# A chunked RWKV-7 scan: GpSimd's mask of the backward inverse levels behind VectorE's running sums, and y of the backward direction on the other two quadrants of TensorE's array

## The chip, the cores and the metric

One NeuronCore of a Trainium2 chip runs the whole program. It has five engines with queues of their own: TensorE (PE in the profile, its weight loads PEld), VectorE (DVE), ScalarE (ACT), GpSimd (POOL) and SyncE (SP), which here only issues DMAs. Engines meet through semaphores. The metric is the device time of the program in microseconds, lower is better.

## What is computed

The reference is an encoder trunk of two layers over 1280 tokens (a prompt of 1024 and a sample of 256) of width 1024: neighbourhood attention, a gated MLP, an RWKV-7 time mixing in both directions, and a second gated MLP. The change lies in the scan of the time mixing. For each of 16 heads of 64 channels and each direction a state S (64 x 64) goes through the tokens:

```python
def _wkv7_step(S, inp):
    r_t, w_t, k_t, v_t, aa_t, bb_t = inp
    sa = jnp.einsum('zbhij,zbhj->zbhi', S, aa_t)
    S = S * w_t[..., None, :] + sa[..., :, None] * bb_t[..., None, :] + v_t[..., :, None] * k_t[..., None, :]
    y = jnp.einsum('zbhij,zbhj->zbhi', S, r_t)
    return S, y
```

z is the direction, forward (0) or backward (1); y of both is added later, in the gate.

## The kernel before

The scan is the function `rwkv_scan`. Two heads make a pair, on partitions 0 to 63 and 64 to 127 (`halves`); there are 8 pairs. The tokens are cut in chunks of C = 64, and U = 4 chunks of each direction make a **group** of W = 256 tokens, 5 to a pair, so NG = 40 groups. For a chunk the recurrence is solved in closed form: products of decayed keys and queries (`gram`), the inverse of a triangular 64 x 64 matrix, built level by level (`inverse`), and then the chain that must go from chunk to chunk: `x_product`, `u_product`, `s_product`, which gives the next state `st`. When a group's chain is done, `y_products` gives y of all its chunks.

Each engine has a hand-written program: a loop over I from -3 (or -4) to NG - 1, in four steps s each. In loop I the chain of group I runs, the inverse of group I + 1, gram and the level masks of group I + 2, decays and keys of group I + 3, and y of group I - 1. One turn of this loop is called a loop here. Every engine does its instructions in the order in which they are issued; only semaphores order engines against each other. What matters for the change, in step s = 1 of a loop:

- TensorE: x, inverse level, u, inverse level, s, `gram` of group I + 2 for z = 1, then `y_products(I - 1)` (L1681 on, matmuls at L1693, L1695 and L1697), then an inverse level. In step 2: x, an inverse level, u, `turn` (transposes of keys and values), and an inverse level that needs the level output of VectorE (L1952).
- VectorE: level outputs, the state output (L1967), `gram_out` for z = 1 (L1912 writes `bm`, which frees GpSimd's mask), a level output, then `sums(I + 3)`: the running sums over the log decays of a group, forward (L1851) and backward (L1852), and L1855 and L1856, which turn the backward one around. L1856 signals `d_cum`. The next level output follows it.
- ScalarE: waits for `d_cum` and takes exponentials (L1769, L1770); it copies y from PSUM (`y_copy`, L1804) and the inverse's products (L1781).
- GpSimd: `directions(I + 3)` (L2000, L2002), `levels(I + 2, 1)` in step 2 (L2019, L2026, L2027), `receptance(I + 3)` in step 3 (L2009, L2010), `bonus_add` (L2036). `levels(G, z)` multiplies the gram block `bm` by the mask of level 0 (L2019), adds the identity (L2026), and multiplies `bm` by the masks of the other five levels, 128 x 1280 elements (L2027), for TensorE's inverse in the next loop.
- SP: loads of a group, then the stores of y (`store_y`, L1514), one DMA for each direction.

A head's matmul of 64 x 64 takes one quadrant of the 128 x 128 array: its input half gives the row half, its output half the column half. y of both directions went from half h to half h, and `y_ps` has one PSUM bank for each z. `side(h, z)` is half h for z = 0 and the other half for z = 1. An fp32 matmul of this kind is two records in the trace.

Of the kernel before, what the change touches and what calls it, by code (L numbers as in the profile page):

```python
# [15 lines left out]
ALU = mybir.AluOpType  # L16
# [3 lines left out]
P = 128  # L20
# [1334 lines left out]
C = 64  # L1355
# [4 lines left out]
Z = 2  # L1360
# [13 lines left out]
def rwkv_scan(nc, rkvl, kks, w0, w2, a0, a2, k_a, r_k, ysc, bsc, consts):  # L1374

    U = 4
    W = U * C
    NS = T // W
    NG = PAIRS * NS
    INV = LEVELS - 1  # L1380
    halves = (slice(0, HD), slice(HD, P))
    with Phase(nc, "sc") as ph:
        ident = ph.sb("ident", [P, P])
        block64 = ph.sb("block64", [P, P])
        eye2 = ph.sb("eye2", [P, Z, C])
# [30 lines left out]
        rec = ph.sb("rec", [P, 4, Z, U, 4, C])  # L1416
        yt = ph.sb("yt", [P, 3, Z, W])
# [10 lines left out]
        nr = ph.sb("nr", [P, 4, Z, 2, U, C])  # L1428
        t0 = ph.sb("t0", [P, 2, Z, 2, U, C])
        vt = ph.sb("vt", [P, 2, Z, U, C])  # L1430
        xs = ph.sb("xs", [P, Z, C])
        tu = ph.sb("tu", [P, 2 * U, Z, C])
        st = ph.sb("st", [P, 2 * U, Z, C])
# [8 lines left out]
        y_ps = low_ps[:, :, 0:W]  # L1442
# [4 lines left out]
        y_stored, b_stored = ph.sems("y_stored", 3), ph.sems("b_stored", 2)  # L1447
# [5 lines left out]
        d_start, d_cum, d_run, d_tb, d_rec, d_bonus, d_two, d_st, a_y = (  # L1453
            ph.sem(x) for x in ("d_start", "d_cum", "d_run", "d_tb", "d_rec", "d_bonus", "d_two", "d_st", "a_y"))
        d_bm, d_gram, d_first, d_t, d_r = (ph.sems(x, Z) for x in ("d_bm", "d_gram", "d_first", "d_t", "d_r"))
        g_kd, g_ab, g_r, g_bt = (ph.sem(x) for x in ("g_kd", "g_ab", "g_r", "g_bt"))
        g_bl, g_r0, g_first = (ph.sems(x, Z) for x in ("g_bl", "g_r0", "g_first"))

        def col_of(z, j):
            return (j if z == 0 else NS - 1 - j) * W  # L1460

        def unit(z, s):
            return s if z == 0 else U - 1 - s

        def group(G):
            return 0 <= G < NG

        def side(h, z):
            return halves[h] if z == 0 else halves[1 - h]
# [8 lines left out]
        with nc.Block() as block:  # L1478
            @block.sync
            def _(sp):  # L1480
                loads = [(ident[:], consts["ident"]), (block64[:], consts["block64"]), (eye2[:], consts["eye2"]),
                         (m_strict[:], consts["m_strict"]), (m_incl[:], consts["m_incl"]), (m_level[:], consts["m_level"]),
                         (keep[:], consts["keep"]), (wa[:, 0], w2), (wa[:, 1], a2)]
                with nc.allow_non_contiguous_dma("parameters by channel"):
                    for i, q in enumerate((w0[0], w0[1], a0[0], a0[1], k_a, r_k)):
                        sp.dma_start(prm[:, i], q.rearrange("(k p) -> p k", p=P)).then_inc(small_in, 16)
                for dst, src in loads:
                    sp.dma_start(dst, src).then_inc(small_in, 16)

                def load(G):  # L1490
                    p, j = divmod(G, NS)
                    s = G % 2
                    if G >= 2:
                        sp.wait_ge(g_r, G - 1)
                        sp.wait_ge(d_rec, G - 1)
                    for z, rows in enumerate(halves):
                        c = col_of(z, j)
                        sp.dma_start(low[rows, s], rkvl[rows, 3 * KT:3 * KT + 2, c:c + W]).then_inc(s_in[s], 16)
                        sp.dma_start(rk[:, s, :, z], rkvl[:, p:p + KT + 1:KT, c:c + W]).then_inc(s_in[s], 16)
                        sp.dma_start(kk[:, s, z], kks[:, p, c:c + W]).then_inc(s_in[s], 16)  # L1500
                    if G >= 4:
                        for z in range(Z):
                            sp.wait_ge(pe_turn[z], G - 3)
                        sp.wait_ge(d_bonus, G - 3)
                    for z in range(Z):
                        c = col_of(z, j)
                        sp.dma_start(vb[:, G % 4, z], rkvl[:, 2 * KT + p, c:c + W]).then_inc(v_in[G % 4], 16)

                def store_y(G):
                    p, j = divmod(G, NS)  # L1510
                    sp.wait_ge(a_y, G + 1)
                    for z in range(Z):
                        c = col_of(z, j)
                        sp.dma_start(ysc[:, p, z, c:c + W], yt[:, G % 3, z]).then_inc(y_stored[G % 3], 16)  # L1514

                for I in range(-4, NG):
                    if group(I + 4):
                        load(I + 4)
                    if I >= 2 and I % NS == 2:
                        p = I // NS  # L1520
                        sp.wait_ge(d_bonus, (p + 1) * NS)
                        sp.wait_ge(g_bt, (p + 1) * 2)
                        sp.wait_ge(d_two, p + 1)
                        sp.dma_start(bsc[:, p], bt[:, p % 2]).then_inc(b_stored[p % 2], 16)
                    if I >= 2:
                        store_y(I - 2)
                store_y(NG - 2)
                store_y(NG - 1)
                for s in range(3):
                    sp.wait_ge(y_stored[s], 32 * len(range(s, NG, 3)))  # L1530
                for s in range(2):
                    sp.wait_ge(b_stored[s], 16 * PAIRS // 2)

            @block.tensor
            def _(pe):
# [145 lines left out]
                def y_products(G):  # L1681
                    pe.wait_ge(a_u, 4 * G + 4)
                    if group(G + 4):
                        pe.wait_ge(a_tanh, G + 5)
                    else:
                        pe.wait_ge(d_bonus, NG)
                        pe.wait_ge(a_turn[0], min(G + 2, NG))
                    for z in range(Z):
                        for s in range(U):
                            u, g = unit(z, s), (4 * G + s) % (2 * U)  # L1690
                            to = slice(u * C, (u + 1) * C)
                            for rows in halves:
                                nc.tensor.matmul(y_ps[rows, z, to], st[rows, g, z], rec[rows, G % 4, z, u, 3], start=True, stop=False)  # L1693
                            for rows in halves:
                                nc.tensor.matmul(y_ps[rows, z, to], tu[rows, g, z], nr[rows, G % 4, z, 0, s], start=False, stop=False)  # L1695
                            for rows in halves:
                                last = nc.tensor.matmul(y_ps[rows, z, to], vt[rows, G % 2, z, s], nr[rows, G % 4, z, 1, s], start=False, stop=True)  # L1697
                    last.then_inc(pe_y, 1)

                def bonus(G):  # L1700
# [34 lines left out]
            def _(act):  # L1735
# [64 lines left out]
                def y_copy(G):  # L1800
                    act.wait_ge(pe_y, G + 1)
                    if G >= 3:
                        act.wait_ge(y_stored[G % 3], 32 * (G // 3))
                    nc.scalar.activation(yt[:, G % 3], y_ps, ACT.Copy).then_inc(a_y, 1)  # L1804

                for I in range(-3, NG):
# [184 lines left out]
            def _(pool):  # L1991
# [17 lines left out]
                    nc.gpsimd.tensor_tensor(rec[:, G % 4, :, :, 0], uc(ab[:]), uc(ex2[:]), ALU.mult)  # L2009
                    nc.gpsimd.tensor_tensor(rec[:, G % 4, :, :, 3], uc(rk[:, G % 2, 0]), ex1_of, ALU.mult).then_inc(g_r, 1)  # L2010

                def levels(G, z):
                    pool.wait_ge(d_bm[z], G + 1)
                    if z == 0 and G >= 3:
                        pool.wait_ge(pe_u, 4 * G - 8)
                    if z == 1 and G >= 1:
                        pool.wait_ge(d_start, G)
                    first = rf[:, G % 3, 0] if z == 0 else r0[:]
                    nc.gpsimd.tensor_tensor(first, bm[:, z], m_level[:, 0, z:z + 1].to_broadcast([P, U, C]), ALU.mult).then_inc(g_first[z], 1)  # L2019
                    if G >= 2:  # L2020
                        pool.wait_ge(pe_p[z], 5 * G - 5)
                    m = m_level[:, 1:LEVELS, z]
                    mask = strided(m, 0, [[Z * C, INV], [0, U], [1, C]])
                    src = strided(bm[:, z], 0, [[0, INV], [C, U], [1, C]])
                    pool.wait_ge(g_first[z], G + 1)
                    nc.gpsimd.tensor_tensor(first, first, eye2[:, z:z + 1].to_broadcast([P, U, C]), ALU.add).then_inc(g_r0[z], 1)  # L2026
                    nc.gpsimd.tensor_tensor(bl[:, G % 2, z], src, mask, ALU.mult).then_inc(g_bl[z], 1)  # L2027

                def bonus_add(G):
# [9 lines left out]
                for I in range(-3, NG):  # L2039
                    for s in range(U):  # L2040
                        if s == 1 and group(I + 2):
                            levels(I + 2, 0)
                        if s == 2 and group(I + 2):
                            levels(I + 2, 1)
                        if s == 1 and group(I + 3):
                            directions(I + 3)
                        if s == 3 and group(I + 3):
                            receptance(I + 3)
                        if s == 0 and group(I + 2):
                            bonus_add(I + 2)  # L2050
# [320 lines left out]
```

## Time and profile before

| | before |
|---|---|
| median of 3 runs (lowest, highest) | 4919.04 us (4917.08, 4932.63) |
| profiled execution, its own time | 4925.97 us |
| its span, first to last instruction | 4924.0 us |
| TensorE, VectorE, ScalarE, GpSimd busy | 4368.1, 1982.0, 1291.8, 1276.4 us |
| mean granted TensorE clock | 0.947 |

Times in the rows are microseconds from the span's start unless marked ns. A timeline row gives start, duration, engine, line, operation, output and inputs, and the count of instructions merged in it; in brackets stands the idle time of the engine before it, with what ended that. "issue" is time in which the engine waited for nothing that the profile shows.

### The profile page before, as it was taken

The numbers are of one execution on the slowest core, as the hardware profiler recorded it, in microseconds if no ns is written. First come the engines' busy times: TensorE is split into PE (matmuls) and PEld (weight loads), VectorE is DVE, ScalarE is ACT, GpSimd is POOL, SyncE is SP. The second block draws the span as 40 slices with busy tenths as digits, with TensorE's granted clock in tenths as the row PEclk, the third lists the DMA queues.
The fourth block names the chain that finished last, engine by engine and source line by source line (L and its number), as shares of the span: only waits on it lengthen the run. The fifth ranks groups of instructions, "written<-read, shape, count | busy, mean of one in ns | idle before, by whom it ended". The sixth has DMA issues, their size and how long they took to land. (4 is left out here: it accounts for less than half of the span.)

```text
span 4924.0 us, 112761 instructions
## 1 busy us (share of the span) xinstructions
PE 4368.1 (89%) x50312; PEld 3680.4 (75%) x50312; DVE 1982.0 (40%) x3380; ACT 1291.8 (26%) x2542; POOL 1276.4 (26%) x794
## 2 busy tenths in 40 slices
PE   3899798999999996997948888888878999999997
PEld 2788766888888885876747777777765888888886
DVE  3011064253242533125156666666644244153341
ACT  2111075211110112335124444444422211011110
POOL 2111132311111124111045445445422321111110
PEclk6899999999999997998979999999999999999998
DMA  3211243312213122221231122121222411312214
GB/s 129 66 58 60 79 118 80 109 39 66 93 39 125 39 78 60 75 70 60 78 86 61 60 73 61 60 69 59 63 77 96 126 40 41 123 39 89 70 48 165
DMA packets 401998, 372.41 MB, mean 76 GB/s; under 512 B 62416, under 2 KB 369872, under 8 KB 399344
## 3 DMA queue, kind: packets, MB, share of 16 engines
q1 hardware_dynamic: 389680, 354.75, 23.2%
q10 hardware_dynamic: 11840, 10.49, 0.6%
q8 instruction: 397, 6.50, 0.6%
q14 instruction: 81, 0.66, 0.0%
HBM read 257.68 MB, written 107.48 MB: 74 GB/s over the span
## 5 line engine op out<-in xcount | busy, mean ns | idle before, releaser
L422 POOL TENSOR_TENSOR f_wlow<-f_raw,f_whigh 128x1024 fp32r<-128x1024 f32 (+1 forms) x152 | 360.1, 2369 | 1670.9 <-ACT f_whigh L493 1670.9
L478 PE MATMUL f_ps<-fx_hh,f_whigh 128*128 128x512 f32 (+1 forms) x2112 | 529.8, 359 | 0.0
L478 PE MATMUL f_ps<-fx_hl,f_whigh 128*128 128x512 f32 (+1 forms) x2112 | 528.7, 358 | 0.0
L478 PE MATMUL f_ps<-fx_hh,f_wlow 128*128 128x512 f32 (+1 forms) x2112 | 528.5, 358 | 0.0
L1603 PE MATMUL sc_inv_ps<-sc_tf,sc_bl 64*64 64x64 f32 x6400 | 281.0, 224 | 158.8 <-DVE sc_tf L1952 120.6
L493 ACT ACTIVATE f_whigh<-f_raw 128x1024 fp32r<-128x1024 f32 (+1 forms) x152 | 156.5, 1030 | 923.2 <-PE f_ps L478 894.9
L478 PEld LDWEIGHTS f_ps<-fx_hl,f_whigh 128*128 128x128 f32 x2112 | 349.1, 189 | 65.3
L478 PEld LDWEIGHTS f_ps<-fx_hh,f_whigh 128*128 128x128 f32 x2112 | 349.4, 189 | 64.7
L478 PEld LDWEIGHTS f_ps<-fx_hh,f_wlow 128*128 128x128 f32 x2112 | 348.8, 189 | 65.2
L478 PE MATMUL f_ps<-mo_oh,f_whigh 128*128 128x512 f32 (+1 forms) x1440 | 360.8, 359 | 25.9 <-POOL f_wlow L422 25.9
L1603 PEld LDWEIGHTS sc_inv_ps<-sc_tf,sc_bl 64*64 64x64 f32 x6400 | 235.6, 136 | 196.8 <-issue 111.6
L478 PE MATMUL f_ps<-mo_ol,f_whigh 128*128 128x512 f32 (+1 forms) x1440 | 360.3, 359 | 0.0
L478 PE MATMUL f_ps<-mo_oh,f_wlow 128*128 128x512 f32 (+1 forms) x1440 | 360.0, 358 | 0.0
L547 DVE TENSOR_TENSOR f_xo<-f_ps,f_xo 128x512 f32<-128x512 f32 x168 | 90.8, 596 | 619.0 <-PE f_ps L478 586.9
L478 PEld LDWEIGHTS f_ps<-mo_oh,f_whigh 128*128 128x128 f32 x1440 | 240.2, 189 | 69.3 <-POOL f_wlow L422 26.6
L478 PEld LDWEIGHTS f_ps<-mo_ol,f_whigh 128*128 128x128 f32 x1440 | 240.2, 188 | 42.7
L478 PEld LDWEIGHTS f_ps<-mo_oh,f_wlow 128*128 128x128 f32 x1440 | 240.0, 188 | 42.9
L1206 PE MATMUL ri_ps<-ri_xh,ri_whigh 128*128 128x512 f32 (+1 forms) x672 | 185.0, 386 | 75.9 <-DVE ri_xl L1322 74.4
L1614 PE MATMUL sc_inv_ps<-sc_pt,sc_rf 64*64 64x64 f32 x5120 | 232.9, 227 | 7.3 <-issue 7.0
L2027 POOL TENSOR_TENSOR sc_bl<-sc_bm,sc_m_level 128x1280 f32<-128x1280 f32 x80 | 233.4, 2918 | 0.0
L1781 ACT ACTIVATE sc_pt<-sc_inv_ps 128x256 f32<-128x256 f32 x320 | 122.8, 384 | 383.0 <-PE sc_inv_ps L1603 382.6
L1206 PEld LDWEIGHTS ri_ps<-ri_xh,ri_whigh 128*128 128x128 f32 x672 | 117.9, 200 | 112.0 <-DVE ri_xl L1322 57.6
(268 smaller groups left out, 8688.4 us busy)
## 6 DMA issues: line engine op xcount, KB each, us to landing
f_xo<-xres SPq DMA_DIRECT2D x64, 640.0 KB, 4.0
xres<-f_xo SPq DMA_DIRECT2D x56, 640.0 KB, 2.9
f_raw<-in_ffn_w_gate SPq DMA_DIRECT2D x44, 512.0 KB
f_raw<-in_ffn_w_up SPq DMA_DIRECT2D x44, 512.0 KB
sc_rk<-rkvl SPq DMA_DIRECT2D x80, 256.0 KB, 3.3
rkvl<-ri_ot SPq DMA_DIRECT2D x28, 640.0 KB, 2.9
f_raw<-in_ffn_w_down SPq DMA_DIRECT2D x32, 448.0 KB
qkv_raw<-in_na_w_qkv SPq DMA_DIRECT2D x24, 512.0 KB, 5.7
```

The costliest lines, as they stand in the source:

```text
L422: nc.gpsimd.tensor_tensor(wlow[:, m % 2, 0:kt], raw[:, 0:kt], whigh[:, m % 2, 0:kt].bitcast(F32), ALU.subtract).then_inc(cut_lo, 1)
L478: last = nc.tensor.matmul(ps[:, m % 2, n, 0:count], w[:, m % 2, k], x[:, k, t0:t0 + count], start=(k == 0 and w is whigh and x is xh), sto ...
L493: nc.scalar.activation(whigh[:, m % 2, 0:kt], raw[:, 0:kt], ACT.Copy).then_inc(cut_hi, 1)
L547: last = nc.vector.tensor_tensor(dst, src, old, ALU.add)
L1206: last = nc.tensor.matmul(ps[:, m % 2, q, 0:count], w[:, m % 2, k], src[:, k, t0:t0 + count], start=(k == 0 and w is whigh and src is xh), ...
L1603: return nc.tensor.matmul(p_ps[z][side(h, z), s * C:(s + 1) * C], bl[rows, G % 2, z, k, s], tf[rows, G % 2, z, s], start=True, stop=True)
L1614: return nc.tensor.matmul(t_ps[z][halves[h], s * C:(s + 1) * C], rf[rows, G % 3, z, s], pt[rows, z, s], start=True, stop=True)
L1781: nc.scalar.activation(dst, src, ACT.Copy).then_inc(a_pt[z], 1)
L2027: nc.gpsimd.tensor_tensor(bl[:, G % 2, z], src, mask, ALU.mult).then_inc(g_bl[z], 1)
```

## The change

In the GpSimd program `levels` is split. `first_level` holds the product of level 0 and the addition of the identity, at the place they had. What is left of `levels`, the mask of the five other levels, waits for z = 1 on `d_cum` of the group whose sums VectorE takes in the same loop; for z = 0 it has no new wait.

In the TensorE program y of direction 1 is written to the other half than it is read from (`side(h, z)`), and the two directions are issued in turn, chunk by chunk, term by term and half by half. ScalarE's copy is as before, so y of direction 1 stands in `yt` with its halves exchanged, and SP stores it in two DMAs of 64 partitions; the counts of `y_stored` go from 32 to 48.

```diff
--- before.py
+++ after.py
@@ -1509,9 +1509,11 @@
                 def store_y(G):
                     p, j = divmod(G, NS)
                     sp.wait_ge(a_y, G + 1)
-                    for z in range(Z):
-                        c = col_of(z, j)
-                        sp.dma_start(ysc[:, p, z, c:c + W], yt[:, G % 3, z]).then_inc(y_stored[G % 3], 16)
+                    c = col_of(0, j)
+                    sp.dma_start(ysc[:, p, 0, c:c + W], yt[:, G % 3, 0]).then_inc(y_stored[G % 3], 16)
+                    c = col_of(1, j)
+                    for h, rows in enumerate(halves):
+                        sp.dma_start(ysc[rows, p, 1, c:c + W], yt[side(h, 1), G % 3, 1]).then_inc(y_stored[G % 3], 16)
 
                 for I in range(-4, NG):
                     if group(I + 4):
@@ -1527,7 +1529,7 @@
                 store_y(NG - 2)
                 store_y(NG - 1)
                 for s in range(3):
-                    sp.wait_ge(y_stored[s], 32 * len(range(s, NG, 3)))
+                    sp.wait_ge(y_stored[s], 48 * len(range(s, NG, 3)))
                 for s in range(2):
                     sp.wait_ge(b_stored[s], 16 * PAIRS // 2)
 
@@ -1685,16 +1687,18 @@
                     else:
                         pe.wait_ge(d_bonus, NG)
                         pe.wait_ge(a_turn[0], min(G + 2, NG))
-                    for z in range(Z):
-                        for s in range(U):
-                            u, g = unit(z, s), (4 * G + s) % (2 * U)
-                            to = slice(u * C, (u + 1) * C)
-                            for rows in halves:
-                                nc.tensor.matmul(y_ps[rows, z, to], st[rows, g, z], rec[rows, G % 4, z, u, 3], start=True, stop=False)
-                            for rows in halves:
-                                nc.tensor.matmul(y_ps[rows, z, to], tu[rows, g, z], nr[rows, G % 4, z, 0, s], start=False, stop=False)
-                            for rows in halves:
-                                last = nc.tensor.matmul(y_ps[rows, z, to], vt[rows, G % 2, z, s], nr[rows, G % 4, z, 1, s], start=False, stop=True)
+                    for s in range(U):
+                        g = (4 * G + s) % (2 * U)
+                        to = [slice(unit(z, s) * C, (unit(z, s) + 1) * C) for z in range(Z)]
+                        for h, rows in enumerate(halves):
+                            for z in range(Z):
+                                nc.tensor.matmul(y_ps[side(h, z), z, to[z]], st[rows, g, z], rec[rows, G % 4, z, unit(z, s), 3], start=True, stop=False)
+                        for h, rows in enumerate(halves):
+                            for z in range(Z):
+                                nc.tensor.matmul(y_ps[side(h, z), z, to[z]], tu[rows, g, z], nr[rows, G % 4, z, 0, s], start=False, stop=False)
+                        for h, rows in enumerate(halves):
+                            for z in range(Z):
+                                last = nc.tensor.matmul(y_ps[side(h, z), z, to[z]], vt[rows, G % 2, z, s], nr[rows, G % 4, z, 1, s], start=False, stop=True)
                     last.then_inc(pe_y, 1)
 
                 def bonus(G):
@@ -1800,7 +1804,7 @@
                 def y_copy(G):
                     act.wait_ge(pe_y, G + 1)
                     if G >= 3:
-                        act.wait_ge(y_stored[G % 3], 32 * (G // 3))
+                        act.wait_ge(y_stored[G % 3], 48 * (G // 3))
                     nc.scalar.activation(yt[:, G % 3], y_ps, ACT.Copy).then_inc(a_y, 1)
 
                 for I in range(-3, NG):
@@ -2009,7 +2013,7 @@
                     nc.gpsimd.tensor_tensor(rec[:, G % 4, :, :, 0], uc(ab[:]), uc(ex2[:]), ALU.mult)
                     nc.gpsimd.tensor_tensor(rec[:, G % 4, :, :, 3], uc(rk[:, G % 2, 0]), ex1_of, ALU.mult).then_inc(g_r, 1)
 
-                def levels(G, z):
+                def first_level(G, z):
                     pool.wait_ge(d_bm[z], G + 1)
                     if z == 0 and G >= 3:
                         pool.wait_ge(pe_u, 4 * G - 8)
@@ -2017,13 +2021,17 @@
                         pool.wait_ge(d_start, G)
                     first = rf[:, G % 3, 0] if z == 0 else r0[:]
                     nc.gpsimd.tensor_tensor(first, bm[:, z], m_level[:, 0, z:z + 1].to_broadcast([P, U, C]), ALU.mult).then_inc(g_first[z], 1)
+                    pool.wait_ge(g_first[z], G + 1)
+                    nc.gpsimd.tensor_tensor(first, first, eye2[:, z:z + 1].to_broadcast([P, U, C]), ALU.add).then_inc(g_r0[z], 1)
+
+                def levels(G, z):
                     if G >= 2:
                         pool.wait_ge(pe_p[z], 5 * G - 5)
+                    if z == 1 and group(G + 1):
+                        pool.wait_ge(d_cum, G + 2)
                     m = m_level[:, 1:LEVELS, z]
                     mask = strided(m, 0, [[Z * C, INV], [0, U], [1, C]])
                     src = strided(bm[:, z], 0, [[0, INV], [C, U], [1, C]])
-                    pool.wait_ge(g_first[z], G + 1)
-                    nc.gpsimd.tensor_tensor(first, first, eye2[:, z:z + 1].to_broadcast([P, U, C]), ALU.add).then_inc(g_r0[z], 1)
                     nc.gpsimd.tensor_tensor(bl[:, G % 2, z], src, mask, ALU.mult).then_inc(g_bl[z], 1)
 
                 def bonus_add(G):
@@ -2039,8 +2047,10 @@
                 for I in range(-3, NG):
                     for s in range(U):
                         if s == 1 and group(I + 2):
+                            first_level(I + 2, 0)
                             levels(I + 2, 0)
                         if s == 2 and group(I + 2):
+                            first_level(I + 2, 1)
                             levels(I + 2, 1)
                         if s == 1 and group(I + 3):
                             directions(I + 3)
```

## Rows read from the trace of the kernel before

**Rows 1.** The page, busy us (share) and instructions of each engine: TensorE's.

```profile
PE 4368.1 (89%) x50312; PEld 3680.4 (75%) x50312; DVE 1982.0 (40%) x3380; ACT 1291.8 (26%) x2542; POOL 1276.4 (26%) x794
```

**Rows 2.** Busy time by stretch, the scan stage; its header row names the columns.

```profile
2472.00:3670.00 1198.00, 953.68 (x31200) 870.44 (x31200) 776.09 (x1825) 471.82 (x1281) 567.48 (x432) 0.96 0.21 62
```

**Rows 3.** VectorE timeline, one late loop: start us, us, engine, line, operation [idle before].

```profile
3045.83 2.88 DVE L1851 TENSOR_TENSOR_SCAN sc_cum<-sc_restart,sc_sg 128x256 f32<-128x256 f32 x1
3048.64 0.66 DVE L1852 TENSOR_TENSOR_SCAN sc_run<-sc_restart,sc_sg 128x256 f32<-128x256 f32 x1
...
3049.41 0.41 DVE L1856 TENSOR_TENSOR sc_cum<-sc_run 128x252 f32<-128x252 f32 x1
3049.74 0.28 DVE L1952 TENSOR_TENSOR sc_tf<-sc_inv_ps,sc_tf 128x128 f32<-128x128 f32 x1
```

**Rows 4.** GpSimd timeline, the same loop.

```profile
3043.71 0.72 POOL L2019 TENSOR_TENSOR sc_r<-sc_bm,sc_m_level 128x256 f32<-128x256 f32 x1
3044.58 0.73 POOL L2026 TENSOR_TENSOR sc_r<-sc_r,sc_eye 128x256 f32<-128x256 f32 x1
3045.27 2.89 POOL L2027 TENSOR_TENSOR sc_bl<-sc_bm,sc_m_level 128x1280 f32<-128x1280 f32 x1
3052.63 1.27 POOL L2009 TENSOR_TENSOR sc_rec<-sc_ab,sc_ex 128x512 f32<-128x512 f32 x1 [4.46 <-ACT sc_exb L1770]
3053.86 1.19 POOL L2010 TENSOR_TENSOR sc_rec<-sc_rk,sc_exb 128x512 f32<-128x512 f32 x1
```

**Rows 5.** TensorE timeline, the same loop: where it resumes behind the sums.

```profile
3050.17 0.27 PE L1603 MATMUL sc_inv_ps<-sc_tf,sc_bl 64*64 64x64 f32 x2 [2.38 <-DVE sc_tf L1952]
```

**Rows 6.** Groups by line, VectorE, scan stage: xcount | busy us, mean ns | idle before.

```profile
L1851 DVE TENSOR_TENSOR_SCAN sc_cum<-sc_restart,sc_sg 128x256 f32<-128x256 f32 x40 | 89.8, 2245 | 9.6 <-ACT sc_sg L1755 9.6
...
L1852 DVE TENSOR_TENSOR_SCAN sc_run<-sc_restart,sc_sg 128x256 f32<-128x256 f32 x40 | 30.5, 763 | 0.0
```

**Rows 7.** Groups by line, VectorE, scan stage: the level outputs.

```profile
L1952 DVE TENSOR_TENSOR sc_tf<-sc_inv_ps,sc_tf 128x128 f32<-128x128 f32 x320 | 92.7, 290 | 234.8 <-PE sc_inv_ps L1614 232.4
```

**Rows 8.** VectorE and GpSimd timelines, the fourth loop.

```profile
2566.57 3.31 DVE L1852 TENSOR_TENSOR_SCAN sc_run<-sc_restart,sc_sg 128x256 f32<-128x256 f32 x1
...
2566.05 3.27 POOL L2027 TENSOR_TENSOR sc_bl<-sc_bm,sc_m_level 128x1280 f32<-128x1280 f32 x1
```

**Rows 9.** VectorE timeline: L1851 in the fifth loop and in the last.

```profile
2593.72 2.88 DVE L1851 TENSOR_TENSOR_SCAN sc_cum<-sc_restart,sc_sg 128x256 f32<-128x256 f32 x1
...
3590.32 2.89 DVE L1851 TENSOR_TENSOR_SCAN sc_cum<-sc_restart,sc_sg 128x256 f32<-128x256 f32 x1
```

**Rows 10.** VectorE timeline, the last loop.

```profile
3593.91 0.41 DVE L1856 TENSOR_TENSOR sc_cum<-sc_run 128x252 f32<-128x252 f32 x1
...
3599.29 0.75 DVE L1864 SCALAR_TENSOR_TENSOR sc_tb<-sc_kd,sc_prm,sc_rk 128x512 f32<-128x512 f32 x1
```

**Rows 11.** TensorE timeline: the first and the last start of one y block.

```profile
3041.64 0.31 PE L1693 MATMUL sc_low_ps<-sc_rec,sc_st 64*64 64x64 f32 x4
...
3044.41 0.22 PE L1697 MATMUL sc_low_ps<-sc_nr,sc_vt 64*64 64x64 f32 x1
```

**Rows 12.** TensorE timeline: an inverse level, first row, and what starts behind it.

```profile
3037.45 0.27 PE L1603 MATMUL sc_inv_ps<-sc_tf,sc_bl 64*64 64x64 f32 x2 [1.05 <-DVE sc_tf L1952]
...
3037.94 0.28 PE L1664 MATMUL sc_chain_ps<-sc_xs,sc_rf 64*64 64x64 f32 x5
```

**Rows 13.** TensorE timeline: the u products of one step.

```profile
3030.94 0.34 PE L1664 MATMUL sc_chain_ps<-sc_xs,sc_rf 64*64 64x64 f32 x8
```

**Rows 14.** Groups by line, TensorE, scan stage: L1603 with its idle time before.

```profile
L1603 PE MATMUL sc_inv_ps<-sc_tf,sc_bl 64*64 64x64 f32 x6400 | 281.0, 224 | 158.8 <-DVE sc_tf L1952 120.6 <-ACT sc_pt L1781 15.0 <-issue 11.5
```

**Rows 15.** TensorE timeline: a stop for issue.

```profile
3012.91 0.38 PE L1678 MATMUL sc_chain_ps<-sc_tu,sc_t 64*64 64x64 f32 x5 [1.02 <-issue]
```

**Rows 16.** One tile's instructions, sc_yt: its stores.

```profile
L1514 SPq DMA_DIRECT2D ysc<-sc_yt x80: 319/432/1956, 2611.5 to 3667.8; - x80
```

**Rows 17.** Waits of SP in the scan stage: waited for: us in total, times, longest us.

```profile
SPq L1495 <- DVE sc_pc L1879: 816.9, 38, 25.7
```

## The prediction, made before the change was run

> **What bounds the kernel now.** I read the page's busy shares first. TensorE is busy 4368.1 of 4924.0 us [rows 1], so a gain must come from TensorE's own work or from its waits. The diff touches only the scan stage (functions inside `rwkv_scan`), so the second view was the busy time by stretch: the scan runs from about 2472 to 3670 us. In those 1198 us TensorE is busy 953.68 at a granted clock of 0.96, and GpSimd is busy 567.48 [rows 2]. About 244 us of the stage are TensorE's idle time.
>
> The third view was the timeline of one late loop, engine by engine. VectorE's first running sum (L1851) stands there with 2.88 us, the second (L1852), the same operation on the same shape, with 0.66 [rows 3]. GpSimd's mask L2027 runs from 3045.27 to 3048.16 [rows 4], and the sum ends at 3048.71, 0.55 us behind it. In each of the 36 loops from the fifth on, the first sum ends 0.54 or 0.55 us after the end of the backward mask, whatever its own start was. So the sum does not run slowly: it stands still while the mask runs. The reader is to see who waits for that. Behind the sums VectorE has L1855, L1856 and the level output L1952 (3049.74), and TensorE resumes at 3050.17 after 2.38 us of idle time that the profile puts on that L1952 [rows 3, 5]. In all 36 loops TensorE resumes 0.34 to 0.36 us after L1856 ends. The wait is on the path.
>
> **Part 1, the mask behind the sums.** The product for level 0 and the addition of the identity (L2019, L2026) keep their place; only L2027 for z = 1 now waits for `d_cum`, which L1856 signals. The first sum has a mean of 2245 ns in 40 runs, the second 763 [rows 6]; clear of GpSimd either takes some 0.66, as L1852 in [rows 3]. The time that goes is 40 x (2.245 - 0.66) + 40 x (0.763 - 0.66) = 63.4 + 4.1 = **67 us**.
>
> Three things are taken off.
> (a) A new clash. With y shorter (part 2) the sum is ready about 1.3 us earlier, at 3045.83 - 1.30 = 3044.53. That is between L2019, which ends at 3044.43, and L2026, which starts at 3044.58 and ends at 3045.31 [rows 4]. The one case of that sort in the trace is the fourth loop: L2027 starts while a first sum runs and is stretched to 3.27 us, and the second sum then stands for 3.31 us, to 0.56 us behind it [rows 8]. Here the second GpSimd operation is only 0.73 long. The first sum ends at 3044.53 + 0.66 = 3045.19; L2026 begins its work about 0.22 before that, as in [rows 8] (a mask of 2.9 us that ends 3.27 behind 2566.05 has its work from 2566.42, and that sum ends at 2566.64), and ends near 3045.7; the second sum ends 0.55 later, 3046.25, against 3045.85 undisturbed: some 0.4 lost. If L2026 gets in first, the loss is 0.7. A first sum lasts 3.44 us less what it starts behind the mask, so with a start 1.30 earlier it meets L2026 where it lasts over 2.14 us now: 23 of the 36 loops, the first and the last among them [rows 9]; 18 at 0.4 and 5 at less, about -9 us.
> The Trainium skill (SBUF — State Buffer, "Who interferes with whom") says that a VectorE instruction with two SBUF inputs and a GpSimd instruction that reads SBUF lock each other out for the whole instruction, and that the one issued first keeps the ports. For VectorE as the loser [rows 3] agree with 2.88 against 0.66 us, for GpSimd as the loser [rows 8] with 3.27 against 2.89; by that rule the first sum would win in this clash and the loss be the 0.4.
> (b) In the first four loops other work still sets the pace, and in some late ones TensorE's wait is a little shorter than the excess (1.95 against 2.2 in one): I take -5 us.
> (c) GpSimd is now busy later. The mask runs from the end of L1856 + 0.1 to + 3.0; the receptance pair L2009, L2010 started 2.81 us after L1856 before (3052.63 against 3049.82) and takes 3055.05 - 3052.63 = 2.42 us [rows 3, 4], so it ends at + 5.45 instead of + 5.23 or, in the fast loops, 4.98. L1864, with two SBUF inputs as the sums have, begins at + 4.97 in the last loop (3599.29 against 3594.32) [rows 10], and within + 5.4 in 21 of the 36. There it will stand until 0.61 behind L2010, ending at 6.06 instead of 5.72: 0.34 x 21 = -7 us, by the 0.55 that the sum of [rows 3] ends behind the mask and 0.06 for the longer operation, because VectorE has no pause from there to the state output that TensorE waits for.
> Nothing else is queued badly: what is behind the new wait on GpSimd is the receptance, which needs exponentials that need `d_cum` anyway, and the mask itself is wanted by TensorE only in the next loop (`inverse(G, 1)`), behind L1864 and all of [rows 4]. The VectorE operations that the mask now lies beside (L1952, the transposes, L1967) have one SBUF input; over half of the 320 L1952 lie beside GpSimd work already, and their mean is 290 ns against the 0.28 of one that doesn't [rows 7, 3]. Part 1: 67 - 9 - 5 - 7 = **46 us**.
>
> **Part 2, y on four quadrants.** A group has 4 chunks x 2 directions x 3 terms x 2 halves = 48 matmuls of 64 x 64, 96 records. Before, each z used only the two diagonal quadrants, and in one loop the block goes from 3041.64 to the last start at 3044.41 [rows 11]: 2.77 us, 28.9 ns a record. Where two z are issued together on all four quadrants, the inverse levels have 32 records from 3037.45 to 3037.94 [rows 12], 15.3 ns each; the u products have 8 in 0.34 us where one alone takes 0.22 [rows 13, 11], so (0.34 - 0.22) / 7 = 17.1 ns. So y takes 96 x 15.3 = 1.47 us (saving 1.30) or 1.64 (saving 1.13). I take 1.30, since the inverse runs as long a row of them: 40 blocks, **52 us**, lower bound 45. No wait lies between gram, y and the next inverse level, so all of it is on TensorE's path, and what follows (ACT's copy of y and of p, then L1952, then the sum) moves up with it; it is this that makes clash (a).
>
> Against it stands the supply of instructions. TensorE stops now and then for "issue": 11.5 us before L1603 alone, and 1.02 us at 3012.91 [rows 14, 15]; over all lines of the stage it is 39 us in 40 loops. The stops follow dense stretches, and y becomes twice as dense while the pause behind the scans, in which supply could catch up, shrinks from 2.4 to under 1 us. No row prices this. Bounds: 0, and one more stop of 1.02 us in each loop, 41 us. I take half, **-20 us**, since now there is one such stop in about every loop and y is the longest dense stretch.
>
> The store of the backward y becomes two DMAs of 64 rows instead of one: one more issue of median 432 ns on SP per group [rows 16]. SP waits 816.9 us in the stage for VectorE before the loads [rows 17], and the stores are the last in its loop, so this costs nothing; without that cover it would be 40 x 0.43 = 17 us. At the end of the stage one such issue may show, 0.4 us.
>
> **The sum**: 46 + 52 - 20 = 78 us. Against the profiled execution's own 4925.97 us (span 4924.0) this gives 4848; that execution was 7 us above the median of the runs, 4919.04, so the forecast is 4919 - 78 = **4841 us**.
>
> **The rivals.**
> A: no price for the supply of instructions, and few clashes. Then 67 - 5 + 52 = 114 at best: 4805, more likely 4815. For it: most dense stretches now pass without a stop. Against: stops of 0.5 to 2 us stand in half of the loops.
> B: y gains nothing, because neighbours in the new order share a row half (h outside, z inside) or because both row halves write one bank. Then only part 1 is left, without (a): 67 - 5 - 7 = 55, less some supply: about 4870. Against it: in [rows 12] the order also puts matmuls of the same row half next to each other, at 15.3 ns.
> The Trainium skill (TensorE: Matmul & The Clock Gate, "Part 3: Packing small matmuls — row/col tiling") says that a weight load overlaps running matmuls only where the row group differs. By that rule half of y's loads would stand exposed; [rows 12] disagree as far as they go.
> C: the supply eats y's gain altogether (a stop of 1 us in each loop and more after the scans): 46 + 52 - 45 = 53, about 4866 to 4880.
> D, slower than before: the four quadrants take turns in this order. Per quadrant a record takes 2 x 28.9 = 57.7 ns; one at a time y would last 96 x 57.7 = 5.5 us, 2.8 more than now, 40 x 2.8 = +111, less part 1 without (a), 55: +56, 4975. It decides from a pace above 43 ns a record, where y's loss of 1.4 us a loop cancels part 1. Nothing in the trace shows such a pace.
> E: the change does not do what it says, say because the sum, clear of the mask, now always stands behind L2026 and L1864 and TensorE finds another wait: within 15 us of before.
>
> **How the numbers follow.** Forecast (both parts, 55 to 98 us gained, 4821 to 4864): 0.60. A: 0.15. B: 0.06. C: 0.13. D: 0.03. E: 0.03. The likeliest gives 4841. The range of 8 in 10 takes in most of A and C: 4808 to 4878. TensorE's clock is in it too: a loop with a stretch at 1.2 GHz lasts 30.5 to 31.8 us against some 28, and about 14 of them may become a few more or fewer. About 0.3% (15 us) is what a measurement of this kernel can tell from no change. Faster by more: 0.94; within: 0.03; slower: 0.03.
>
> **What would show it.** L1851 under 0.7 us in the loops where it starts clear of GpSimd, and under 1.5 elsewhere; L2027 for z = 1 starting 0.1 us behind L1856; TensorE's wait on L1952 before L1603 cut from 2.38 to under 1 us; y's block at 1.5 to 1.7 us; "issue" in the stage at about 60 us; a loop of about 26 us instead of 28. The prediction is wrong where y's pace stays at 28.9 ns, where "issue" grows past 80 us, or where TensorE's clock falls in every loop.

## The result, and the profile after

The changed kernel takes 4867.92 us (median of 4 runs, 4861.30 to 4877.74) against 4921.22 before, a ratio of 0.989 with a 95% interval of 0.9871 to 0.9909: by the ratio 54 us less. The forecast was 4841, with a range of 4808 to 4878. The profiled execution took 4869.98 us, with a span of 4867.9 and a mean granted clock of 0.954.

The first view is VectorE's timeline of a late loop, then GpSimd's, of the changed kernel (start, duration, engine, line; L1855 and L1856 are the two sums, L1859 and L1860 turn the backward one around, L1860 signals `d_cum`, L2025 adds the identity, L2035 is the mask).

```profile
3049.76 0.65 DVE L1855 TENSOR_TENSOR_SCAN sc_cum<-sc_restart,sc_sg 128x256 f32<-128x256 f32 x1
3050.33 1.15 DVE L1856 TENSOR_TENSOR_SCAN sc_run<-sc_restart,sc_sg 128x256 f32<-128x256 f32 x1
3051.51 0.17 DVE L1859 COPY sc_cum<-sc_run 128x4 f32<-128x4 f32 x1
3051.59 0.41 DVE L1860 TENSOR_TENSOR sc_cum<-sc_run 128x252 f32<-128x252 f32 x1
```

```profile
3049.05 0.72 POOL L2023 TENSOR_TENSOR sc_r<-sc_bm,sc_m_level 128x256 f32<-128x256 f32 x1
3049.85 1.08 POOL L2025 TENSOR_TENSOR sc_r<-sc_r,sc_eye 128x256 f32<-128x256 f32 x1
3052.14 2.91 POOL L2035 TENSOR_TENSOR sc_bl<-sc_bm,sc_m_level 128x1280 f32<-128x1280 f32 x1 [1.22 <-DVE sc_cum L1860]
...
3056.24 1.17 POOL L2014 TENSOR_TENSOR sc_rec<-sc_rk,sc_exb 128x512 f32<-128x512 f32 x1
```

The first sum, 2.88 us in [rows 3], is at 0.65. The clash that the prediction drew up stands there as drawn: L1855 starts as L2023 ends (3049.76 and 3049.77) and ahead of L2025, L2025 is stretched to 1.08, and the second sum ends at 3051.48, 0.55 behind L2025's end at 3050.93. The mask starts 0.14 us behind the end of L1860. Over the stage (groups by line, as in [rows 6]):

```profile
L1855 DVE TENSOR_TENSOR_SCAN sc_cum<-sc_restart,sc_sg 128x256 f32<-128x256 f32 x40 | 30.9, 773 | 9.8 <-ACT sc_sg L1759 9.8
L1856 DVE TENSOR_TENSOR_SCAN sc_run<-sc_restart,sc_sg 128x256 f32<-128x256 f32 x40 | 30.8, 771 | 0.0
L1868 DVE SCALAR_TENSOR_TENSOR sc_tb<-sc_kd,sc_prm,sc_rk 128x512 f32<-128x512 f32 x40 | 32.7, 816 | 1.2
```

The sums together fell from 89.8 + 30.5 = 120.3 us to 61.7, by 58.6. TensorE's y block, 2.77 us between first and last start in [rows 11], goes in one loop from 3046.76 to 3048.32:

```profile
3046.76 0.27 PE L1695 MATMUL sc_low_ps<-sc_rec,sc_st 64*64 64x64 f32 x1
...
3048.32 0.22 PE L1701 MATMUL sc_low_ps<-sc_nr,sc_vt 64*64 64x64 f32 x2
```

That is 1.56 us, 16.3 ns for each of the 96 records (the 28.9 before was reckoned in the same way). The mean block is 1.91 us against 2.87, since some now have a stop inside. So both parts do what they say, for 58.6 us of standing and some 38 us of y, 97 in all, and 54 us came. What took the rest stands in TensorE's waits. These are its four longest of the 940 us from 2590 to 3530, first for the changed kernel, then for the kernel with part 1 alone, e1_mask_only (waited for: us in total, times, longest us; L1605 there is L1603 here):

```profile
PE sc_inv_ps L1605 <- DVE sc_tf L1956: 47.4, 92, 1.0
PE sc_inv_ps L1605 <- issue: 19.6, 28, 1.7
PE sc_inv_ps L1616 <- issue: 18.3, 21, 1.4
PE sc_inv_ps L1605 <- ACT sc_pt L1785: 13.0, 43, 0.4
```

```profile
PE sc_inv_ps L1603 <- DVE sc_tf L1952: 46.4, 86, 1.6
PE sc_inv_ps L1603 <- ACT sc_pt L1781: 13.2, 46, 0.6
PE sc_inv_ps L1603 <- issue: 10.5, 16, 1.8
PE sc_inv_ps L1614 <- issue: 9.3, 12, 1.4
```

The waits for VectorE and ScalarE are the same in both. Over all lines of the scan stage, "issue" is 39.0 us before, 52.7 with part 1 alone, and 100.5 with both; TensorE's waits for everything else are 205.5, 156.9 and 157.0.

The stops grew by 61.5 us, more than the 43 that are missing. The granted clock gave part of it back: of the 940 us, 46.1 were at 1.2 GHz before, 10.2 in the changed kernel and 3.4 in e1_mask_only. From one L1860 (L1856 before) to the next, the 36 late loops last 28.44 us in the mean before, 26.80 after and 26.72 in e1; those without any stretch at 1.2 GHz (26, 34 and 35 of them) last 27.94, 26.64 and 26.66. That is 59 and 62 us over 36 loops, of which 47 and 46 stand at the full clock. So an estimate from these loops is that some 12 us of the gain of the change, and some 16 of that of e1, came with the clock. The loops of one kind differ by 0.6 to 1.1 us among themselves, so it is a rough one.

### The profile page after: what moved, and what is told of

Read it like the earlier page. It is cut to its first block and busy times, and to the rows that moved or that the text cites. A ratio compares the mean times of both kernels' runs of the same rounds, so it can differ in the third digit from the quotient of the medians.

```text
span 4867.9 us, 112762 instructions
## 1 busy us (share of the span) xinstructions
PE 4311.4 (89%) x50312; PEld 3614.9 (74%) x50312; DVE 1928.2 (40%) x3380; ACT 1292.7 (27%) x2542; POOL 1279.7 (26%) x794
## 5 line engine op out<-in xcount | busy, mean ns | idle before, releaser
L1605 PE MATMUL sc_inv_ps<-sc_tf,sc_bl 64*64 64x64 f32 x6400 | 283.0, 223 | 105.3 <-DVE sc_tf L1956 59.8
L1605 PEld LDWEIGHTS sc_inv_ps<-sc_tf,sc_bl 64*64 64x64 f32 x6400 | 237.8, 135 | 140.0 <-ACT sc_pt L1785 72.1
L2035 POOL TENSOR_TENSOR sc_bl<-sc_bm,sc_m_level 128x1280 f32<-128x1280 f32 x80 | 233.0, 2913 | 81.9 <-DVE sc_cum L1860 81.9
L1616 PEld LDWEIGHTS sc_inv_ps<-sc_pt,sc_rf 64*64 64x64 f32 x5120 | 185.4, 134 | 23.7 <-issue 23.5
```

What stands on the lines that cost most here:

```text
L1605: return nc.tensor.matmul(p_ps[z][side(h, z), s * C:(s + 1) * C], bl[rows, G % 2, z, k, s], tf[rows, G % 2, z, s], start=True, stop=True)
L1616: return nc.tensor.matmul(t_ps[z][halves[h], s * C:(s + 1) * C], rf[rows, G % 3, z, s], pt[rows, z, s], start=True, stop=True)
```

## The experiments

All times are medians, the ratios are to the kernel before on the same chip with their 95% intervals. Two such ratios differ clearly from about 0.0024, 12 us.

**e1_mask_only**, only the GpSimd part:

```diff
+                def first_level(G, z):
...
                 def levels(G, z):
+                    if z == 1 and group(G + 1):
+                        pool.wait_ge(d_cum, G + 2)
```

> Part 1 alone: GpSimd's mask behind the sums, y as before. Theory S (TensorE's supply of instructions takes back part of each gain): the first running sum falls from a mean of 2245 ns to under 700, about 60 us of standing go, and stops for issue in the scan stage rise from 39 us to some 60: about 4880 us. Rival P (nothing is taken back, the 0.989 of the whole change is all that both parts are worth on the path): issue stays near 39 us and the time is about 4866, as good as the whole change. Rival Y (y is the part that brings the gain): over 4905.

4867.09 us, 0.9889 (0.9872 to 0.9906): the whole gain of the change. P's time came, with issue (52.7 us) between what P and S expected, and with some 16 us that came with the clock. First sum 678 ns, second 711, no clash.

**e2_y_only**, only the TensorE and SP part:

```diff
-                                nc.tensor.matmul(y_ps[rows, z, to], st[rows, g, z], rec[rows, G % 4, z, u, 3], start=True, stop=False)
+                                nc.tensor.matmul(y_ps[side(h, z), z, to[z]], st[rows, g, z], rec[rows, G % 4, z, unit(z, s), 3], start=True, stop=False)
```

> Part 2 alone: y on four quadrants, the mask where it was. The y block falls from 2.77 to about 1.57 us between first and last start. If the two parts are independent, that is 1.2 x 40 = 48 us: about 4873. If the parts hang together (the sum becomes ready 1.2 us earlier, but still stands until 0.55 us behind the mask, whose time y does not set), only the last loops gain: first sums of 3.4 to 4 us instead of 2.9, and 4910 to 4921 us.

4920.68 us, 0.9993 (0.9982 to 1.0004): nothing. The parts hang together, though not quite by the rows expected. The sum is ready earlier, but L1860, which ends the work on the sums, still ends behind the mask in all 36 late loops. Rows of three of e2's loops on VectorE (L1859 is the small copy behind the sums, 0.17 us when it is clear), and the mask of the second:

```profile
3021.83 2.77 DVE L1855 TENSOR_TENSOR_SCAN sc_cum<-sc_restart,sc_sg 128x256 f32<-128x256 f32 x1
3024.52 0.66 DVE L1856 TENSOR_TENSOR_SCAN sc_run<-sc_restart,sc_sg 128x256 f32<-128x256 f32 x1
...
3049.23 0.81 DVE L1855 TENSOR_TENSOR_SCAN sc_cum<-sc_restart,sc_sg 128x256 f32<-128x256 f32 x1
3049.96 3.31 DVE L1856 TENSOR_TENSOR_SCAN sc_run<-sc_restart,sc_sg 128x256 f32<-128x256 f32 x1
...
3077.55 2.68 DVE L1859 COPY sc_cum<-sc_run 128x4 f32<-128x4 f32 x1
```

```profile
3049.44 3.28 POOL L2031 TENSOR_TENSOR sc_bl<-sc_bm,sc_m_level 128x1280 f32<-128x1280 f32 x1
```

In 13 of the 36 loops the first sum stands; in 15 it slips in before the mask and the second stands, until 0.55 us behind 3052.72; in 8 both sums slip in and the copy stands, until 0.03 us behind the mask's end. The loops of the three sorts last 28.2, 28.4 and 28.3 us, as before (28.4). The sums have 125.8 us of stage time, more than before. The stops for issue are here too, 74.1 us in the stage against 39.0, while the waits for everything else stay at 207.9: with the mask where it was, they fill time that y gave up and that was not on the path.

**e4_before_two_terms**, the kernel before with a third of its y matmuls left out (`vt` times `nr`):

> The kernel before without the third term of y (y is not the reference's): the block gets 32 x 28.9 ns = 0.92 us shorter in each loop. If y's length is on the path there: 37 us less, about 4884. If the sum stands until the mask's end anyway: only the last loops gain, under 10 us, with at most 10 more from fewer instructions: 4903 to 4916.

4928.12 us, 1.0008 (0.9996 to 1.002). Not even a few microseconds came of it. It bears e2 out from the other side: TensorE's wait for the level output, 120.6 us in [rows 14], takes in what y gave up.

```profile
PE sc_inv_ps L1603 <- DVE sc_tf L1950: 160.1, 140, 3.7
```

There was one price more: the granted clock of 2590 to 3530 is 0.95 against 0.98 before, with TensorE busy 757 us of the 940 instead of 778. It doesn't hide a gain of 37: the loops without a stretch at 1.2 GHz (9 here, 26 before) last 27.86 us against 27.94, 3 us over 36 loops.

**e3_after_two_terms**, the same left out of the changed kernel:

> The changed kernel without the third term of y (values times the masked products): 32 of the 96 records of each y block are left out, 64 fewer instructions in a group, so y is not the reference's. Theory P (the engine's pace counts): 32 x 16.4 ns x 40 = 21 us less than the changed kernel, about 4847. Theory S (instructions count): from the trace, packets of 16 KB of instructions never follow each other in less than 3.37 us, that is 13.2 ns an instruction; 64 x 13.2 ns x 40 = 34 us less, about 4834, with issue well under 100 us.

4825.56 us, 0.9805 (0.9788 to 0.9822): 42 us below the changed kernel, where the records' own pace is worth 21 and their instructions 34. Issue is at 72.8 us. S's forecast (34) is the nearer. So y is on the path in the changed kernel, as it wasn't before, and what it costs there is nearer to a price by the instruction than to its pace.

**e5_order**, the loops over h and z exchanged, so that neighbours inside a term never share a row half:

```diff
-                        for h, rows in enumerate(halves):
-                            for z in range(Z):
+                        for z in range(Z):
+                            for h, rows in enumerate(halves):
```

> The changed kernel with the four quadrants of a y term in the other order: z outside, h inside, so that neighbouring matmuls never share a row half inside a term. If sharing a row half costs TensorE anything, the undisturbed y block falls from 1.57 us between first and last start (16.4 ns a record) to 1.47 (15.3, the inverse's pace). If not, it stays at 1.55 to 1.60. The time stays within 10 us of the changed kernel in either case.

4867.83 us, in a single run. Two blocks last 1.45 us and the next shortest 1.55, against 1.56 and then 1.57 to 1.59; e7 below, with the changed kernel's order, has two of 1.41. So no price for shared row halves shows. The Trainium skill (TensorE: Matmul & The Clock Gate, "Part 3: Packing small matmuls — row/col tiling") says that a weight load overlaps running matmuls only where the row group differs. What that would cost here does not show, at 16.3 ns a record in one order and 16.1 in the other.

**e6_before_narrow12** and **e7_after_narrow12**, 24 matmuls of four columns more in each loop, ahead of the transposes of direction 0:

```diff
+                        for i in range(12):
+                            for rows in halves:
+                                nc.tensor.matmul(turn_ps[z][rows, 0, 4 * i:4 * i + 4], rec[rows, r, z, 0, 0], ident[rows, rows.start:rows.start + 4],
+                                                 start=True, stop=True)
```

> The kernel before with 24 more matmuls of four columns (48 records, 96 instructions) in each loop, ahead of the transposes of direction 0, whose region they write first. TensorE then stands idle for 1 to 2.4 us behind the transposes in most loops, and the added work lasts at most 48 x 28.9 ns = 1.39 us. Theory P (pace and waits alone): hidden, 0 to 15 us more. Theory S (supply of instructions, 13.2 ns each): the stops for issue rise by 10 to 40 us over the 39, and part of it shows: 10 to 35 us more.

> The same 24 short matmuls in the changed kernel, where no pause is left to hide them. Theory P: their own duration, at most 1.39 us x 38 = 53 us, less if short ones run faster. Theory S: 96 x 13.2 ns x 38 = 48 us at the least, whatever their pace, and issue above 100 us. It separates the two only together with the next run.

e6: 4931.50 us, 1.0014 (1.0004 to 1.0023), 7 us more, and issue 47.1 us. TensorE's waits for everything else fell from 205.5 to 152.2 us, by what the new matmuls take (48 records in 1.32 us where nothing stops them, 53 us in 40 loops): the pauses hide them, and S's 10 to 35 did not come. The clock was a little higher than before (20.5 us at 1.2 GHz against 46.1); at the full clock a loop is 0.4 us longer, some 14 us in all, so S's lower end is not ruled out. e7: 4934.29 us, 1.003 (1.0018 to 1.0042), 66 us above the changed kernel. That is more than P's 53 at most, and it fits S's 48 at least, but issue, which S had above 100 us, fell to 71.2. The granted clock of 2590 to 3530 fell from 0.99 to 0.94, with 112.6 us at 1.2 GHz against 10.2. Only 8 of the 36 loops have no such stretch; they last 27.43 us against 26.64, 28 us over 36 loops. By this estimate from few loops about half of the 66 is the clock, and the run doesn't separate P from S.

**e8_after_narrow48**, 96 of them:

> The changed kernel with 96 short matmuls (192 records, 384 instructions) in each loop at that place. They are a dense stretch longer than what is in store, so their average pace is that of the supply: by theory S 384 x 13.2 ns = 5.1 us for the stretch, about 26.4 ns a record, with stops for issue inside it, and 190 to 200 us more in all. By theory P the stretch has no stops, and lasts 192 x the pace of an undisturbed short record, which the rows show between the stops.

5238.27 us, 1.0644 (1.0626 to 1.0662). It decides nothing: the granted clock of 2590 to 3530 is at 0.84, and in the stretches at 1.2 GHz the short matmuls go at 53 ns a record, slower than the 26 that S puts on the supply.

**e9_mask_state** (on part 1 alone) and **e10_after_state** (on the changed kernel) take 32 real records out of a loop: the state's own term leaves the s products.

```diff
-                            nc.tensor.matmul(s_ps[rows, z], ident[rows, rows], st[rows, g, z], start=True, stop=False)
...
+                        last = nc.scalar.activation(stc[:, z], st[:, g % (2 * U), z], ACT.Copy, scale=pc[:, G % 4, z, u:u + 1])
...
-                    nc.vector.tensor_tensor(st[:, (g + 1) % (2 * U)], s_ps, scale, ALU.mult).then_inc(d_st, 1)
+                        last = nc.vector.scalar_tensor_tensor(st[:, (g + 1) % (2 * U), z], s_ps[:, z], pc[:, G % 4, z, u:u + 1], stc[:, z], ALU.mult, ALU.add)
```

> Part 1 alone (the mask behind the sums, y on two quadrants), and the state's own term leaves TensorE: the scaled state is made by ScalarE and added by VectorE, which takes 32 records (64 instructions and some 0.9 us of matmuls) out of each loop and adds two small ScalarE operations and one VectorE operation to each step. Against e1_mask_only: 32 records were worth 42 us in e3_after_two_terms; less 4 x 0.1 us a loop on VectorE: 20 to 40 us less, 4827 to 4847. If TensorE's supply is not what binds: at most 10 us less.

> The changed kernel with the same 32 records a loop taken out. Theory S (with y on four quadrants the supply of instructions is what binds, so y's gain comes back as soon as there are fewer instructions): 10 to 30 us below e9_mask_state, and 30 to 50 below the changed kernel, 4817 to 4838. Rival W (y's pace is worth nothing at all, because another wait ends last behind y): equal to e9_mask_state within 5 us.

e9: 4841.02 us, 0.9837 (0.982 to 0.9854), 26 us below e1, inside the 20 to 40 expected. e10: 4836.37 us, 0.9825 (0.9808 to 0.9842), 32 below the changed kernel, and the fastest that computes the reference. But it is only 5 below e9, which is inside the intervals: y's pace is still worth next to nothing, and S's 10 to 30 was wrong. W's reason is not borne out either. From 2472 to 3540 the waits for other engines are 149.8 us in e9 and 145.7 in e10, while issue goes from 39.7 to 88.4: again some 49 us of stops for y's some 38.

**e11_after_spread**, the changed kernel with y in three pieces, and **e12_after_spread_state**, both:

```diff
+                        if s == 1:
+                            y_products(I - 1, range(0, 2))
                         inverse(I + 1, 3 * s)
                         if group(I):
                             u_product(I, s)
+                        if s == 1:
+                            y_products(I - 1, range(2, 3))
```

> The changed kernel, its y in three pieces instead of one block: chunks 0 and 1 ahead of the inverse level in which TensorE stands about 1 us for VectorE, chunk 2 ahead of the next, chunk 3 where the block was. The instructions are the same in number, the dense block is gone and lies in pauses. Theory S: stops for issue fall from 100 us to 60 to 80, and the time by 15 to 40 us, 4828 to 4853. If the stops depend on the number of instructions alone: issue stays near 100 us and the time within 10 us of the changed kernel.

> Both: y in pieces in the pauses, and the state's own term off TensorE. If they add up, 50 to 80 us below the changed kernel: 4788 to 4818, the fastest of all. If VectorE becomes the bound (it gets four more small operations a loop and loses no work), no better than the better of e10_after_state and e11_after_spread.

e11: 4862.11 us, 0.9874 (0.9857 to 0.989), 8 us below and inside the intervals. From 2472 to 3540 the pauses took some of it (waits for others 131.8 to 119.2 us), but issue stayed at 96.9, against 94.3 in the changed kernel. Both numbers are those of the rival, that the stops depend on the number of instructions alone, and S's 15 to 40 us did not come. The inverse levels around the pieces are as dense as y, so it may be that the dense stretch was moved and not thinned; no run tests that. e12: 4839.68 us, 0.9833 (0.9815 to 0.9851), no better than e10, with issue at 99.8 us in the same stretch: the two did not add up.

## Why the prediction was right, and where its sum was not

*The standing sum* was right in mechanism, place and size. Put at 67 us less 9 for the clash, it measured 58.6 in the rows, and 64.8 without the clash in e1. In time, the rival B had 55 less some supply for part 1 alone, and e1 gave 4925.62 x 0.0111 = 55. That this agrees to the microsecond is luck: 13.7 us more of stops took from it, and some 16 us came with the clock, which the sum did not have.

*Clash (a)* was right: some 0.4 us drawn up for a fast loop, 0.5 in the one shown; means of 773 and 771 ns against 660 make 40 x 0.224 = 9 us, as put. *(c)* was not: L1868 has a mean of 816 ns against 805, 0.4 us in all instead of 7. GpSimd is later as predicted (the receptance ends 5.4 us behind L1860 above), but VectorE comes to L1868 later too: within 5.4 us of L1860 in 1 of the 36 loops instead of 21. In e1, with fewer stops of TensorE, it is 8 of 36, and the mean of L1868 is 859, 2 us in all; that the stops are what delays it is not shown.

*y's pace* was right: 1.30 us a block put, 1.21 measured undisturbed. *y's worth* was the step that failed, "all of it is on TensorE's path". Before, it was not on the path: in e2 and e4 what follows y waits for the mask's end in all 36 loops, and GpSimd's time, not y's, sets that. The prediction had that row, the constant 0.55 us behind the mask whatever the sum's own start, and didn't turn it on y. For both parts together the step is true, and e3 shows it (42 us for a third of the records); what failed there is the next term.

*The supply* was taken at -20, with 41 as the bound, and measured 61.5 us more of stops than before, 13.7 of them with part 1 alone and the other 48 with y. The prediction's own list has it as wrong where "issue" grows past 80 us, and it grew to 100.5. This is the mis-sized term, and with it the rival C (the supply eats y's gain, "about 4866 to 4880", 0.13) is the case that came, at 4868. Counted from each y block's start to 9 us behind, from 2580 to 3535 us, the stops are 4.6 us before, 15.5 in e1 and 55.8 in the changed kernel; the 40 between the last two are about y's gain, returned within a third of a loop. One such stop; it ends some 2 us behind its y block:

```profile
3423.53 0.27 PE L1605 MATMUL sc_inv_ps<-sc_tf,sc_bl 64*64 64x64 f32 x1 [1.44 <-issue]
```

That these stops are waits for instructions still being fetched is inferred from the trace: the instruction queue moves packets of 16 KB, and of the 242 gaps over 0.25 us of the changed kernel from 2590 to 3530, 123 end 1.2 to 1.75 us after such a packet's end, where chance would give some 30; these 123 hold 97 us. In e1 they are 82, with 57 us. Of the stops that the profile calls "issue" nearly all are of this sort: 121 of 125, with 90.8 of their 92.4 us, in the changed kernel, and 54 of 56 before. There are 216 such packets in the 940 us, for 54,626 matmuls and weight loads, 253 to a packet. They never follow each other in less than 3.24 us in any of the runs, which by an estimate of 256 instructions to a packet is some 13 ns for one, 26 for a record with its weight load. Their mean distance is 4.35 us, so by this reading the supply is short in stretches only, not over the loop. Two quadrants ask for a record each 28.9 ns and stay just under that; four ask each 16.3 and run ahead of it, on what is in store. This fits where the stops stand, and e3's 42 us. As a forecast theory S missed e1's time, e6, e10, e11, e12 and the stops of e7, so its sizes are not to be relied on. All of it is an inference: no run changed the supply itself, and whether the 3.24 us is a fixed pace or the latency of one packet asked for at a time stays open.

*Clock*: the prediction had it in its range and not in its sum. Before, 10 of the 36 late loops have a stretch at 1.2 GHz; from one first sum to the next they last 28.9 to 31.8 us, a wider span than the 30.5 to 31.8 read there. After, 2 have one, and the granted clock of 2590 to 3530 went from 0.98 to 0.99. It gave some 12 us, by the estimate above.

*The store* in two DMAs cost nothing that shows, though a half takes longer to issue (median 597 ns) than a whole (432 in [rows 16]):

```profile
L1516 SPq DMA_DIRECT2D ysc<-sc_yt x80: 445/597/1867, 2609.6 to 3609.7; - x80
```

So the number was right with luck in it. y's 52 us did not come, the stops were three times what was put down, the 7 us of (c) did not come either, and the clock gave what nobody had counted; 78 us forecast, 54 measured. The range held because it took in most of C; the likeliest case was not the one that came.

## What to carry to other kernels

When an operation's duration varies while its end keeps a constant distance to another engine's instruction, it is standing, and a gain in what stands ahead of it on the path is worth nothing until that instruction moves: ask this of every part of a change, alone and with the others. A faster issue of the same small matmuls was worth nothing here where the stops for issue grew with it; look at "issue" behind the densest stretches first, and cut the number of matmuls (32 fewer records of some 780 a loop gave 26 us in e9 and 32 in e10) before cutting the time of each. Price two parts of one change singly and together, and look at the clock in both before calling a difference the work's.

## What the runs showed of the hardware

The running sum, a VectorE operation with two SBUF inputs, and a GpSimd operation exclude each other in both directions: 2.88 us instead of 0.66 for the sum, 1.08 instead of 0.73 and 3.28 instead of 2.90 for GpSimd, with 0.54 to 0.56 us from the end of the GpSimd operation to the recorded end of a sum behind it. A copy of 128 x 4 in SBUF, with one input, stood in the same way in 8 loops of e2: 2.68 us instead of 0.17, to 0.03 us behind the mask's end. Four quadrants took fp32 matmuls of 64 x 64 at 15.3 to 16.3 ns a record, with no price for neighbours that share a row half; in dense stretches stops for issue came with it, and instruction packets of 16 KB came no closer than 3.24 us in any run. Matmuls of four columns lowered TensorE's granted clock in the changed kernel (0.99 to 0.94 with 24 a loop, to 0.84 with 96) but not in the kernel before (0.98 to 0.99 with 24), so such a probe has to be read with the clock beside it.
